# First mixer: compression and query rotation drawn into the third projection chunk, memory keys and values behind them

## The reference

```python
h = rms_norm(x, g[0])
z = h @ ev_w_in                      # fox q, k, v, decay; sparse q; kc, vc; ks, vs; kw, vw; gates
# 8 fox heads: causal attention with a decay term
# 8 sparse heads, two key groups, each the gated sum of three attentions:
#   over compressed keys: gelu(blocks(kc) + pos @ w1) @ w2, the same for vc (15 blocks of 32 tokens)
#   over selected blocks ks, vs; over a window kw, vw (rotated keys); with 256 tokens both see all
y = concat(fox, sparse) @ ev_w_out
x = x + rms_norm(y, g[1])
# later, in each of the two layers l: memory attention with
k, v = rms_norm(mem, mem_norm_g[l]) @ ca_wk[l], ... @ ca_wv[l]
```

## Time and profile before

| what | value |
|---|---|
| median of 3 runs | 2107.32 us (2105.61 to 2108.77) |
| the profiled execution's own span | 2102.9 us |
| PE matmul busy | 2028.6 us, 96% |
| DVE busy | 1253.8 us, 60% |
| ACT busy | 1045.6 us, 50% |
| POOL busy | 140.9 us, 7% |
| granted TensorE clock, mean | 0.981 |

### The profile page before, as it was taken

How to read it: one execution, slowest core, us unless ns; L and a number is a source line. 1 busy time by engine, 2 the same in 40 slices (tenths; PEclk the granted TensorE clock), 3 DMA queues, 4 the chain that set the end, 5 groups by cost and what they waited for, 6 DMA issues and landing times.

```text
span 2102.9 us, 26995 instructions
## 1 busy us (share of the span) xinstructions
PE 2028.6 (96%) x9980; PEld 1673.4 (80%) x9980; DVE 1253.8 (60%) x1890; ACT 1045.6 (50%) x1698; POOL 140.9 (7%) x146
## 2 busy tenths in 40 slices
PE   7988899999889999999999999999999999999999
PEld 6875688887768888888778788888888877888887
DVE  5646755567764556455767865556455675865544
ACT  5644644355664445445456645435444556555343
POOL 0000100000000000000402200000000312120000
PEclk9987999999999999999999999999999999999999
DMA  7530466554335555555552545655555653435552
GB/s 273 156 116 12 142 197 192 188 190 141 99 122 181 194 185 180 182 195 168 153 192 77 180 160 181 192 188 180 183 196 182 184 170 121 152 129 179 192 181 99
DMA packets 247145, 346.13 MB, mean 165 GB/s; under 512 B 26148, under 2 KB 180072, under 8 KB 247016
## 3 DMA queue, kind: packets, MB, share of 16 engines
q1 hardware_dynamic: 245768, 342.65, 50.4%
q0 software_dynamic: 544, 1.29, 0.3%
q10 hardware_dynamic: 704, 0.48, 0.1%
HBM read 343.32 MB, written 2.33 MB: 164 GB/s over the span
## 4 chain that ended last, share of the span: by engine, by line
PE 89%; DVE 4%; ACT 2%; issue 2%; POOL 1%; DMA 1%; SPq 0%; ACTq 0%; DVEq 0%; POOLq 0%
PE bank L697 26%; PE bank L699 26%; PE bank L698 26%; PE bank L973 2%; PE bank L1293 1%; PE bank L1101 1%; PE bank L632 1%; ACT w_hi L529 1%; PE bank L1433 1%; POOL gain L2698 1%; PE bank L1151 1%; DVE w_lo L511 1%; PE bank L2104 1%; DMA raw<-in_ev_w_in 1%; DVE jobstat L1020 0%
## 5 line engine op out<-in xcount | busy, mean ns | idle before, releaser
L511 DVE TENSOR_TENSOR w_lo<-raw,w_hi 128x2048 fp32r<-128x2048 f32 (+6 forms) x505 | 739.7, 1485 | 416.1 <-ACT w_hi L529 415.8
L697 PE MATMUL bank<-w_hi,h_hi 128*128 128x512 f32 (+3 forms) x1872 | 739.8, 395 | 15.3 <-issue 5.1
L529 ACT CAST w_hi<-raw 128x2048 fp32r<-128x2048 f32 (+6 forms) x505 | 618.1, 1253 | 263.0 <-PE bank L699 259.9
L698 PE MATMUL bank<-w_lo,h_hi 128*128 128x512 f32 (+3 forms) x1904 | 733.6, 385 | 0.0
L699 PE MATMUL bank<-w_hi,h_lo 128*128 128x512 f32 (+3 forms) x1872 | 725.0, 387 | 0.0
L697 PEld LDWEIGHTS bank<-w_hi,h_hi 128*128 128x128 f32 x1872 | 356.0, 190 | 87.6 <-issue 7.8
L698 PEld LDWEIGHTS bank<-w_lo,h_hi 128*128 128x128 f32 x1904 | 362.7, 190 | 63.8
L699 PEld LDWEIGHTS bank<-w_hi,h_lo 128*128 128x128 f32 x1872 | 355.5, 190 | 69.6
L697 PE MATMUL bank<-w_hi,ff_hi 128*128 128x512 f32 x528 | 206.3, 391 | 0.0
L699 PE MATMUL bank<-w_hi,ff_lo 128*128 128x512 f32 x528 | 205.6, 389 | 0.0
L698 PE MATMUL bank<-w_lo,ff_hi 128*128 128x512 f32 x528 | 205.5, 389 | 0.0
(11 more groups left out here) (326 smaller groups left out, 1680.5 us busy)
## 6 DMA issues: line engine op xcount, KB each, us to landing
raw<-in_ffn_w SPq DMA_DIRECT2D x176, 512.0 KB, 4.7
raw<-in_w_in SPq DMA_DIRECT2D x48, 1024.0 KB, 5.3
raw<-in_ffn_w SPq DMA_DIRECT2D x44, 1024.0 KB, 4.9
raw<-in_ffn_wg SPq DMA_DIRECT2D x44, 512.0 KB, 4.0
raw<-in_ffn_wu SPq DMA_DIRECT2D x44, 512.0 KB, 5.0
raw<-in_ffn_wd SPq DMA_DIRECT2D x22, 1024.0 KB, 4.9
raw<-in_od_w_in SPq DMA_DIRECT2D x12, 1024.0 KB, 5.1
raw<-in_w_out SPq DMA_DIRECT2D x8, 1024.0 KB, 5.0
```

Source lines behind the costliest of these rows:

```text
L511: dve.tensor_tensor(lo_[:, cs], raw_[:, cs], hi[:, cs].bitcast(F32), ALU.subtract).then_inc(*dve_did.up())
L529: act.copy(hi[:, cs], raw_[:, cs]).then_inc(*act_did.up())
L697: pe.matmul(out, x_hi, u.hi[:, k, cols_], start=start, stop=False)
L698: pe.matmul(out, x_hi, u.lo[:, k, cols_], start=False, stop=False)
```

## The change

The weight stream is put in the new order: both compression weights directly behind the projection's, then all four memory units, layer by layer. `sparse_queries` takes its mark from the second chunk, in which its last column lies, and is called after the seventeenth projection step. From the nineteenth projection step on, each is followed by a step of `compress()`, six in all; behind the projection come `sparse_keys()`, the remaining three steps of `compress()`, and the transposes of sparse queries and keys, after which "turned" and "short" are both set. The four halves of the memory work follow, each its turn and then its multiplication, all in the places 0 to 3 of h_hi and h_lo. `do` of group 4 now runs the filler until "short"; that of group 6 is gone.

```diff
--- before.py
+++ after.py
@@ weight_stream @@
             units += gemm_units(a["ev_w_in"][0], FOX_CHUNKS + NSA_CHUNKS)
-            later = memory_units(a["ca_wk"][1], a["ca_wv"][1])
-            units += memory_units(a["ca_wk"][0], a["ca_wv"][0]) + later[0:1]
             for m in "kv":
                 w1 = a[f"ev_cmp_w1_{m}"][0].rearrange("(k p) n -> p k n", p=P)
                 units.append(Unit((CMP_BLOCK // 2, P), lambda v, w1=w1: [(v, w1)], split=False))
-            units += later[1:2]
+            for m in range(DEPTH):
+                units += memory_units(a["ca_wk"][m], a["ca_wv"][m])
@@ sparse_queries @@
-                before = there[NSA_CHUNKS[-1][0]]
+                before = there[NSA_CHUNKS[1][0]]
@@ side @@
                 HALF = KD // 2
+                compressing = None
                 for n, _ in enumerate(gemm_steps(h_in, KD, NSA_CHUNKS, evac, ready)):
                     yield True
                     if n == 11:
                         rstd_rows(gate, rs[:, 28:30])
                         mem_marks["normed"] = pool_did.now()
-                    if n == 19:
-                        yield from memory_turn(0, 0, 0)
-                yield from memory_turn(0, HALF, HALF)
-                sparse_queries()
-                yield from memory_multiply(0, 0, 0)
+                    if n == 16:
+                        sparse_queries()
+                        compressing = compress()
+                    if n > 17:
+                        next(compressing)
+                        yield True
                 sparse_keys()
-                yield from memory_turn(1, 0, 0)
-                yield from memory_multiply(0, HALF, HALF)
+                yield from compressing
                 groups = []
...
                 there["turned"] = groups[-1]
-                compressing = compress()
-                for _ in range(4):
-                    next(compressing)
-                    yield True
-                yield from memory_multiply(1, 0, 0)
-                yield from memory_turn(1, HALF, 0)
-                yield from compressing
                 there["short"] = Marks(pe_did.now(), there["turned"].act, there["compressed"], pool_did.now())
-                yield from memory_multiply(1, HALF, 0)
+                for m in range(DEPTH):
+                    for k0 in (0, HALF):
+                        yield from memory_turn(m, k0, 0)
+                        yield from memory_multiply(m, k0, 0)
@@ even_mixer @@
-            groups[FOX_G]["do"] = lambda: (until("turned"), fill(4))
-            groups[FOX_G + 2]["do"] = lambda: until("short")
+            groups[FOX_G]["do"] = lambda: until("short")
```

## The result

The changed kernel takes 2119.53 us (median of 4, 2117.87 to 2120.93) against 2106.53 us of the kernel before in the same session: 1.0063 times as long, 95% interval 1.0049 to 1.0078. Forecast were 2113.4 us, with a range of 2100.5 to 2121. The sign was right, and so were the mechanisms but for one wait that the forecast didn't have; the size was less than half of it: +6.1 forecast, +13.0 measured.

The account below looks back on a forecast made before the run. Matmul work on PE was taken to set the pace to 124.8 us, the softmax chain from 155. Terms: -0.4 us to the end of iteration 3, +5.9 and +0.6 in the sparse groups: +6.1, 2113.4 us, range 2100.5 to 2121.

Parts of the forecast that it names:

- (a): Compression's inner products: the 4.09 us wait from a mark read late (stale) and the half clock behind it go, -14.6 us.
- (b): Up to iteration 3: six multiply steps and one turn of transposes move out to the sparse groups, -9.1 us.
- (c): Behind the second inner product: PE newly waits for the gelu, held by position copy, rotations and table loads, +5.7 us.
- (d): Memory turns directly before their multiplications: three waits of 1.8, 5.4 and 2.4 us laid bare, +9.6 us.
- R1: Rival, faster: the turns don't stall, so (d) and its two dips, 13.0 us, are gone: 2100.4 us; chance 0.20.
- (e): Clock up to iteration 3: falls at the products (1.7), behind (c) (2.9) and twice behind (d) (3.4), +8.0 us.
- (f): Sparse groups, iterations 4 to 7: moved work and a turn in iteration 5 lengthen 15.6 us to 21.5, +5.9 us.
- (g): Iterations 8 to 11: four weight pieces from iterations 4 to 7 come there one each, +0.6 us.
- R2: Rival, no difference: the sparse groups swallow the moved work, (f) and (g) between 0 and 1: 2107.4 us; chance 0.20.
- R3: Rival, slower: after wait (c) the clock stays low and iteration 2's multiplies run at 1.2 GHz, 2118.9 us; chance 0.10.

Follow-up runs that it names:

- experiment 1: Kernel before, with the first inner product waiting only for the DVE copies of its own windows, not all DVE work given by then: 2099.88 us, 0.9972 times the kernel before.
- experiment 5: The combined kernel: changed kernel with the weighted sum waiting on its copies' own marks, turns one multiplication ahead, gelu ahead of the rotations: 2097.21 us, 0.9961 times kernel before.
- experiment 6: Changed kernel with copies' own marks and gelu ahead, memory work between the steps as before, nothing dealt out over the sparse groups: 2099.62 us, 0.9967 times kernel before.
- experiment 4: Changed kernel with the gelu written out ahead of the rotations and sigmoid of the sparse keys: 2115.4 us, 1.0046 times the kernel before.
- Experiment 3: Changed kernel with each memory turn written out one multiplication ahead: 2100.89 us, 0.9976 times the kernel before.
- experiment 2: Changed kernel with the weighted sum waiting for its probabilities' copies by their own marks, not the bank's mark: 2118.52 us, 1.0058 times the kernel before.
- experiment 7: Experiment 5's kernel with other step counts, so that 16 memory steps instead of 8 reach the sparse groups: 2095.7 us, 0.9954 times the kernel before.
- experiment 8: Changed kernel with compression as one block behind the projection again, rotations and sigmoid ahead of it, memory work last: 2123.56 us, 1.0083 times the kernel before.

## Why the prediction was right, and where its size was off

(a) Right for the wait, and for the trace of the changed kernel: the products take 7.4 us, nothing waits before them. But as a reason it was wrong. I had put the 20 us at half clock down to the stale mark; experiment 1 shows that with 0.88 us of waiting the products still take 11.43 us. In the changed kernel they came through at full clock, with a projection step between them, and the clock fell only behind the second. That was partly luck: in experiments 5 and 6 the same order did not keep the clock. The products also take 7.4 us where half of 13.87 had been counted, 0.4 more.

(b) As counted.

(c) 5.7 forecast, 5.72 measured, released by the gelu; experiment 4 shows that the cause is the rotations and the sigmoid written out ahead of it.

(d) 1.8, 5.4 and 2.4 forecast, 2.22, 5.79 and 3.49 measured: 11.5 for 9.6. Experiment 3 shows that these and the fourth are the change's loss. Of R1 I had said that without (d) and its dips the change would be faster, at 2100.4; with turns that don't stall 2100.9 was measured. That the two numbers meet is luck: R1 took 13.0 us off a forecast that was 6.1 too low, experiment 3 took 18.6 off the measured time. The fourth was the step that failed: I let the turn in iteration 5 cost 2 us, for DVE's share, and saw nobody waiting for it. A weighted sum did, by a mark that had come to mean something else (4.39 us), and without that mark the next transposes would have waited 2.35 (experiment 2).

(e) 8.0 forecast. Three stretches of work at about half clock are 113.9 to 119.6, 137.4 to 143.4 and 151.4 to 156.6 (the last two by stretch):

```profile
137.40:143.40 6.00, 5.92 (x14) 4.68 (x15) 2.27 (x7) 0.43 (x1) 0.00 (x0) 0.52 0.00 0
151.40:156.60 5.20, 5.16 (x12) 3.80 (x12) 1.74 (x3) 0.00 (x0) 0.00 (x0) 0.50 0.02 7
```

Their 16.9 us cost half of that, some 8.4. The 1.7 us for the products themselves did not come, the stretch behind (c) cost its 2.9, and each of the two dips behind (d) 2.6 to 3 instead of 1.7. So the sum came out by two errors that nearly cancel.

Up to iteration 4 the sum was -0.4 and the trace says +3.2: 1.9 from (d), 0.4 from (e), 0.4 from the products of (a), and 0.9 that I can't assign.

(f) +5.9 forecast, +9.95 measured: the mis-sized term, above even its own "nothing hidden" of 9.1. It was 19.5 us of full-clock work and 2 for the turn in iteration 5. The work was right: the stretch from 157.6 has PE busy for 21.04 us at a mean clock of 0.93, which is 1.8 us lost and 19.2 of full-clock work, and the short waits of the softmax chain are gone. But in place of the 2 us there are 4.6 of still PE, 4.39 of them the sum's wait for the turn, and the 1.8 of half clock: 6.4. Iteration 5 took 9.2 us (162.82 to 172.00) where it had taken 4.4 (159.13 to 163.54). (g) 0.6 forecast, 1.7 measured.

R2 fell: the sparse groups took 9.95 us for 9.1 moved. Rid of the turn they hid some 3 of 11 us (experiments 3 and 5), and nothing of eight steps more (experiment 7). R3's time (2118.9) is nearly the measured one, but its mechanism isn't in the trace: the clock is 0.84 in the microsecond from 119 and 1.00 in the next, and the first multiplication (123.48) runs at full clock. The Trainium skill ("ScalarE: Activation LUTs", What ACT_TABLE_LOAD costs) adds a drain of about 1380 ns to each switch to another set; it isn't in this trace either: by the estimate with it the wait would have been 8.5 us, and it is 5.72.

The profiled spans of experiment 8 and of the changed kernel are the same (2118.6 and 2118.5 us) although the medians are 4 us apart: the first is its fastest execution of four (2120.49 us of 2120.49 to 2125.47), the second is 0.9 above its median, and from L2141 to the output projection the mean granted clock is 0.87 in the first and 0.82 in the second. What stays open: what decides when the clock falls within the products, and whether the 2.4 us between experiments 5 and 6 are the dealing out or the wait of 3.42 us. Iterations 4 to 7 take 23.5 us in experiment 5 and 15.2 in 6, 8.3 more for 11.0 us of steps, which speaks for the dealing out; the wait alone would make up as much.

The version with more steps in the sparse groups beats both kernels: 2095.7 us, 23.8 less than the changed one and 0.9954 times the kernel before. That it beats the combined kernel isn't shown.

## What to carry to other kernels

Work that fills another engine's gaps must bring its own lead: a step that hands over between PE, ACT and DVE (here a turn before its multiplication) should be written out one whole unit of other work ahead, or the filler makes gaps of its own, and here the clock fell in two of three of them. Take a mark where the instruction is written out and keep it; one that is read later, from a counter or from a buffer that has been handed on, waits for whatever came between. Before moving work into a stage with idle PE, check whether the other engines leave room there: PE's idle time in a stage paced by another chain is not all free: here about 3 of 11 us went in unseen, and nothing of the next 7.

## What the runs showed of the hardware

I had expected TensorE's clock to fall in waits. With the fp32 products of 45 columns PE was busy without a gap and the granted clock still fell from 1.00 to 0.50 after some 2.6 us (experiment 1, from 125.48) and after some 3.3 us (experiment 5, from 100.40), and in the kernel before it never rose in 13.4 us. With one projection step of 1 us between the halves the same 64 passes ran at full clock to their end in the changed kernel (99.77 to 108.2), but not in experiments 5 and 6, where the clock came down with the first half. So the order of the instructions alone doesn't tell whether the clock stays up.

A table load is carried out before the wait of its own activation where that has a single wait (105.10, under the product, in experiment 4), and behind it where it has several: L2026 waits 4.27 us, then loads, then begins 1.30 us later (ACT of the changed kernel in order of time).

```profile
110.64 1.28 ACT L2026 ACT_TABLE_LOAD   x1 [4.27 <-DVE z L1738]
111.94 0.24 ACT L2026 ACTIVATE stat<-z 128x48 f32<-128x48 f32 x1
112.20 1.28 ACT L2126 ACT_TABLE_LOAD   x1
```

The sigmoid (L2026) has three waits in the kernel, the gelu one. That their number is the cause is read from few places and wasn't tried.
